# Moving four of sixteen weighted sums per head from TensorE to VectorE in the first token tile of a product-key expert layer

## The reference

```python
def block(xb):                      # 128 tokens at a time
    q = (xb @ w_q).astype(F32).reshape(PEER_BLOCK, PEER_HEADS, 2, half)
    s1 = jnp.einsum("thd,hnd->thn", q[:, :, 0], k1.astype(F32))
    s2 = jnp.einsum("thd,hnd->thn", q[:, :, 1], k2.astype(F32))
...
    idx = jnp.take_along_axis(cand_i, pos, axis=-1)
    g = jax.nn.softmax(top_s, axis=-1)
    u = down[idx]
    act = jax.nn.gelu(jnp.einsum("thkd,td->thk", u, xb).astype(F32), approximate=False)
    return jnp.einsum("thk,thkd->td", (g * act).astype(xb.dtype), up[idx])
```

## Time and profile before

| what | value |
|---|---|
| median of 3 runs | 3074.2 us |
| lowest and highest | 3073.37 and 3075.46 us |
| the profiled execution | 3077.88 us |
| its span (first to last instruction) | 3076.1 us |
| TensorE busy | 2693.7 us, 88% |
| VectorE busy | 1747.6 us, 57% |
| ScalarE busy | 881.3 us, 29% |
| GpSimd busy | 1157.1 us, 38% |
| gathers | 536.90 MB, 41.7% of the span of 16 DMA engines |

### The profile page before, as it was taken

One profiled execution on the slowest core, in us unless ns is written; L12 is line 12 of the kernel. 1 busy time (PEld: TensorE's weight loads), 2 busy tenths in 40 slices (PEclk: granted clock), 3 DMA queues, 4 the chain that ended last, 5 costly groups with the idle time before them and its releaser, 6 DMA issues.

```text
span 3076.1 us, 29817 instructions
## 1 busy us (share of the span) xinstructions
PE 2693.7 (88%) x10970; PEld 1857.5 (60%) x10970; DVE 1747.6 (57%) x3667; ACT 881.3 (29%) x1677; POOL 1157.1 (38%) x763
## 2 busy tenths in 40 slices
PE   6999999989989999899978899988777777777776
PEld 4999899977668888788837755543323233322222
DVE  5666762032747604322175477767777777777665
ACT  3111132134542224222142333333222222222221
POOL 1222233223934444423110355545444444444441
PEclk8999999989999999999988999999999999999999
DMA  6455431212025523212200489999999999999996
GB/s 244 158 182 176 162 127 57 62 62 76 22 69 169 173 96 94 91 62 69 71 0 22 150 339 409 411 427 427 427 427 427 427 427 427 427 427 426 427 427 288
DMA packets 125231, 722.07 MB, mean 235 GB/s; under 512 B 14864, under 2 KB 16144, under 8 KB 58288
## 3 DMA queue, kind: packets, MB, share of 16 engines
q0 software_dynamic: 73728, 536.90, 41.7%
q1 hardware_dynamic: 35920, 127.74, 12.1%
q10 hardware_dynamic: 15456, 55.80, 5.6%
HBM read 718.29 MB, written 2.10 MB: 234 GB/s over the span
## 4 chain that ended last, share of the span: by engine, by line
PE 58%; DMA 27%; DVE 9%; ACT 3%; issue 2%; POOL 1%; SPq 0%; ACTq 0%; DVEq 0%; POOLq 0%
PE acc L619 14%; PE acc L620 14%; PE acc L621 14%; DMA wring<-in_peer_rows,squares 9%; DMA hid<-in_peer_rows,squares 8%; PE sums L1120 5%; DMA arena<-in_peer_rows,squares 4%; DMA resid<-in_peer_rows,squares 3%; PE acc L1120 3%; PE sums L552 1%; DMA modw<-in_peer_rows,squares 1%; DVE hid L2534 1%; DVE squares L1924 1%; ACT hid L1179 1%; PE acc L843 1%
## 5 line engine op out<-in xcount | busy, mean ns | idle before, releaser
L2699 POOL TENSOR_TENSOR wring_parts<-wring,wring_parts 128x1024 fp32r<-128x1024 f32 (+1 forms) x215 | 524.2, 2449 | 1180.8 <-ACT wring_parts L1179 1180.6
L619 PE MATMUL acc<-hid_parts,wring_parts 128*128 128x384 f32 (+1 forms) x2152 | 796.2, 370 | 48.6 <-DVE hid_parts L1871 19.6
L621 PE MATMUL acc<-hid_parts,wring_parts 128*128 128x384 f32 (+1 forms) x2152 | 777.2, 361 | 0.0
L620 PE MATMUL acc<-hid_parts,wring_parts 128*128 128x384 f32 (+1 forms) x1656 | 598.6, 361 | 0.0
L619 PEld LDWEIGHTS acc<-hid_parts,wring_parts 128*128 128x128 f32 x2152 | 407.9, 190 | 116.5 <-issue 50.2
L621 PEld LDWEIGHTS acc<-hid_parts,wring_parts 128*128 128x128 f32 x2152 | 407.5, 189 | 38.5
L1179 ACT ACTIVATE wring_parts<-wring 128x1024 fp32r<-128x1024 f32 (+1 forms) x215 | 223.1, 1040 | 514.0 <-DMA wring<-in_w_ffn_out 196.7
L620 PEld LDWEIGHTS acc<-hid_parts,wring_parts 128*128 128x128 f32 x1656 | 314.9, 190 | 32.9 <-issue 5.5
L2711 POOL DMA_INDIRECT arena<-in_peer_rows,squares x180 | 200.5, 1114 | 244.8 <-PE acc L1120 153.4
L1179 ACT ACTIVATE hid<-hid 128x2 f32<-128x2 f32 (+2 forms) x293 | 67.1, 229 | 764.6 <-DVE arena L2534 237.6
L2711 POOL DMA_INDIRECT wring<-in_peer_rows,squares x158 | 176.7, 1118 | 199.3 <-PE acc L1120 144.2
(11 more groups left out here) (422 smaller groups left out, 4284.1 us busy)
## 6 DMA issues: line engine op xcount, KB each, us to landing
wring<-in_w_ffn_in SPq DMA_DIRECT2D x88, 512.0 KB, 4.7
modw<-in_w_ada ACTq DMA_DIRECT2D x56, 512.0 KB, 3.6
modw<-in_w_mod ACTq DMA_DIRECT2D x48, 512.0 KB, 3.8
wring<-in_w_ffn_out SPq DMA_DIRECT2D x32, 512.0 KB, 3.5
wring<-in_w_in SPq DMA_DIRECT2D x28, 512.0 KB, 3.4
wring<-in_w_mix_in SPq DMA_DIRECT2D x18, 512.0 KB, 3.4
wring<-in_peer_w_q SPq DMA_DIRECT2D x16, 512.0 KB, 5.7
wring<-in_w_ffn_out SPq DMA_DIRECT2D x16, 384.0 KB, 3.1
```

Of the source, the lines that this page charges most:

```text
L619: nc.tensor.matmul(o, wh, high, start=first, stop=False)
L620: nc.tensor.matmul(o, wh, low, start=False, stop=False)
L621: return nc.tensor.matmul(o, wl, high, start=False, stop=last)
L2699: nc.gpsimd.tensor_tensor(Wlor[:, p, 0:blocks, 0:cols], Wlo[:, p, 0:blocks, 0:cols], Whir[:, p, 0:blocks, 0:cols], ALU.subtract).then_inc( ...
```

## The change

Of each head 0 to 6 the picks 1, 5, 9 and 13 (28 picks, the list `BY_VECTOR`) are no longer summed by TensorE. VectorE multiplies the up row by its weight and adds it to a running sum. The first is a `tensor_scalar` that starts the sum, the other 27 are `scalar_tensor_tensor`. The sum of 128x1024 floats lies over constants that this stage no longer reads (from `dup0` on). TensorE and ScalarE skip these 28 picks; the remaining picks are renumbered by `tensor_picks`, for the counts of `diag_ready` and `up_used` and for the choice of the diag buffer. A gather that reuses the pair of such a pick waits for a new semaphore, `vector_used`. After tile 0 `finish` adds VectorE's sum to the PSUM sum in one more instruction.

```diff
+BY_VECTOR = [i * PEER_K + s for i in range(7) for s in (1, 5, 9, 13)]
+def tensor_picks(n):
+    return n - sum(m < n for m in BY_VECTOR)
...
             def weighted(i, first, stop):
...
-                    at = n % SLOTS
-                    pe.wait_ge(diag_ready, n + 1)
+                    if n in BY_VECTOR:
+                        continue
+                    at, d = n % SLOTS, tensor_picks(n)
+                    pe.wait_ge(diag_ready, d + 1)
...
             def expert_weights(i, b):
...
+                    if n in BY_VECTOR:
+                        continue
+                    d = tensor_picks(n)
+                    if d >= N_DIAG:
+                        act.wait_ge(up_used, d - N_DIAG + 1)
...
+            def vector_pick(i, s):
+                n = i * PEER_K + s
+                if n in BY_VECTOR:
+                    k = BY_VECTOR.index(n)
+                    up, weight = pair[PAIR_OF[n]][:, D:2 * D], p_w[:, s:s + 1]
+                    dve.wait_ge(weights_ready, i * (PEER_K // BATCH) + s // BATCH + 1)
+                    if k == 0:
+                        V.tensor_scalar(vector_sum, up, weight, None, ALU.mult).then_inc(vector_used, 1)
+                    else:
+                        dve.wait_ge(vector_used, k)
+                        V.scalar_tensor_tensor(vector_sum, up, weight, vector_sum, ALU.mult, ALU.add).then_inc(vector_used, 1)
...
             def finish(t):
...
+                if t == 0:
+                    dve.wait_ge(vector_used, len(BY_VECTOR))
+                    link(V.tensor_tensor(vector_sum, vector_sum, products, ALU.add))
+                    products = vector_sum
...
                 weights(i, 0)
                 dot(i, 2)
+                vector_pick(i, 1)
...
                 weights(i, 2)
                 dot(i, 6)
+                vector_pick(i, 5)
...
             def gather(n):
...
+                before = PAIR_FREE[n]
+                if before is not None and before in BY_VECTOR:
+                    pool.wait_ge(vector_used, BY_VECTOR.index(before) + 1)
+                elif before is not None:
+                    pool.wait_ge(up_used, tensor_picks(before) + 1)
```

More of the change, by code:

```diff
@@ L124 @@
 MORE_PAIRS = {75: 7, 76: 8, 83: 9, 107: 10, 108: 11, 120: 12}
+BY_VECTOR = [i * PEER_K + s for i in range(7) for s in (1, 5, 9, 13)]
+BY_TENSOR = [_n for _n in range(N_PICKS) if _n not in BY_VECTOR]
+def tensor_picks(n):
+    return n - sum(m < n for m in BY_VECTOR)
 PAIR_OF, PAIR_FREE, PAIR_USE = [], [], []
@@ L130 @@
     PAIR_OF.append(_slot)
-    PAIR_FREE.append(_last.get(_slot, -1) + 1)
+    PAIR_FREE.append(_last.get(_slot))
     PAIR_USE.append(PAIR_OF.count(_slot))
@@ L511, in build @@
         dots_done, gelu_ready, weights_ready = sem("dots_done"), sem("gelu_ready"), sem("weights_ready")
-        diag_ready, up_used = sem("diag_ready"), sem("up_used")
+        diag_ready, up_used, vector_used = sem("diag_ready"), sem("up_used"), sem("vector_used")
+        at = CONST["dup0"][0]
+        vector_sum = cst[:, at:at + D]
         ssq_ready, fstd_ready, fin_ready = sem("ssq_ready"), sem("fstd_ready"), sem("fin_ready")
@@ L1116, in weighted @@
                 for n in range(i * PEER_K + first, i * PEER_K + stop):
-                    at = n % SLOTS
-                    pe.wait_ge(diag_ready, n + 1)
+                    if n in BY_VECTOR:
+                        continue
+                    at, d = n % SLOTS, tensor_picks(n)
+                    pe.wait_ge(diag_ready, d + 1)
                     for hf in range(2):
-                        mm = nc.tensor.matmul(o[:, hf, :], diag[n % N_DIAG], pair[PAIR_OF[n]][:, D + hf * 512:D + (hf + 1) * 512],
+                        mm = nc.tensor.matmul(o[:, hf, :], diag[d % N_DIAG], pair[PAIR_OF[n]][:, D + hf * 512:D + (hf + 1) * 512],
                                               start=(at == 0), stop=(at == SLOTS - 1))
@@ L1734, in expert_weights @@
                 for n in range(first, first + BATCH):
-                    if n >= N_DIAG:
-                        act.wait_ge(up_used, n - N_DIAG + 1)
-                    run(diag[n % N_DIAG], ident, ACT.Copy, scale=p_w[:, n % PEER_K:n % PEER_K + 1]).then_inc(diag_ready, 1)
+                    if n in BY_VECTOR:
[3 more added lines that the diff above has]
+                        act.wait_ge(up_used, d - N_DIAG + 1)
+                    run(diag[d % N_DIAG], ident, ACT.Copy, scale=p_w[:, n % PEER_K:n % PEER_K + 1]).then_inc(diag_ready, 1)
             def final_std(t):
@@ L2550, in finish @@
                     emptied(dve, UNIT["rows"] + w)
-                dve.wait_ge(up_used, (t + 1) * SLOTS)
-                V.tensor_tensor(sum_, total[:, :, :].rearrange("p a n -> p (a n)"), g2row,
-                                ALU.mult).then_inc(tile_read, 1)
+                dve.wait_ge(up_used, tensor_picks((t + 1) * SLOTS))
+                products = total[:, :, :].rearrange("p a n -> p (a n)")
+                if t == 0:
+                    dve.wait_ge(vector_used, len(BY_VECTOR))
+                    link(V.tensor_tensor(vector_sum, vector_sum, products, ALU.add))
+                    products = vector_sum
+                V.tensor_tensor(sum_, products, g2row, ALU.mult).then_inc(tile_read, 1)
                 dve.wait_ge(tile_read, CREDIT + t + 1)
@@ L2600, in head @@
                 dot(i, 10)
+                vector_pick(i, 9)
                 if more:
@@ L2614, in head @@
                 dot(i, 14)
+                vector_pick(i, 13)
                 if more:
@@ L2629, in first_head @@
                 dot(0, 2)
+                vector_pick(0, 1)
                 best_pairs(1)
@@ L2643, in first_head @@
                 dot(0, 6)
+                vector_pick(0, 5)
                 key_numbers(1)
@@ L2656, in first_head @@
                 dot(0, 10)
+                vector_pick(0, 9)
                 best_pairs(2)
@@ L2670, in first_head @@
                 dot(0, 14)
+                vector_pick(0, 13)
                 key_numbers(2)
@@ L2708, in gather @@
                     pool.wait_ge(idx_ready, n // PEER_K + 1)
-                if PAIR_FREE[n]:
-                    pool.wait_ge(up_used, PAIR_FREE[n])
+                before = PAIR_FREE[n]
[3 more added lines that the diff above has]
+                    pool.wait_ge(up_used, tensor_picks(before) + 1)
                 nc.gpsimd.indirect_dma_start(pair[PAIR_OF[n]], None, a["peer_rows"],
```

## The result

The changed kernel is slower: its median is 3090.89 us (3085.75 to 3095.99, 9 runs) against 3074.2 us. The ratio over all runs is 1.0049 with a 95% interval of 1.0033 to 1.0064, so 15 us (the two medians lie 16.7 us apart). The forecast was 3072 us, within 0.2%, range to 3079. It was wrong in sign and in size.

What follows compares the result with a forecast made beforehand. The prediction took DMA to bound the kernel, with only DMA time lost before 2000 us winnable. 3077.9 us (profiled) - 3 + 1 = 3075.9, with profiling 3.7 us above the median, so 3072 us, range 3064 to 3079.

Steps and rivals of the forecast that it cites:

- Only lost DMA time can be won: Before 2000 us: DMA paces everything later, so at most 9.0 us in head 0 and 5.6 us behind it.
- are nearly tied: Heads 1 to 3: per head TensorE needs 41.0 us and DMA 41.8 us.
- the waits of GpSimd for TensorE: 1775 to 2000 us: GpSimd waited 86.9 us for pairs TensorE had not yet freed, so DMA starved.
- TensorE, 3 us won: Behind head 0: 28 picks at 1.72 us taken off TensorE win 3 us, bounds 0 to 5.6.
- Head 0, 1 us lost: Head 0: sums delay dots and diags, 1 us lost; bounds 9.0 us won and 4.9 us lost.
- The query that was to cover sum 9: Head 0: diags delayed by sums 5 and 9 cost nothing while query 6 or 7 covers them for 5.87 us.
- Heads 1 to 3, where the 3 us were to be won: Heads 1 to 3: smaller backlog behind the second query, VectorE's idle time hiding most of its 4.9 us per head.
- Heads 4 to 6 and `finish`, 0: Late heads and the final addition: 12 sums, 15 us, and one 1.22 us addition hidden by VectorE's room, cost 0.
- The price of a sum: VectorE, each sum: 1.22 us, about 4.0 us when meeting a low part of GpSimd, one or two more meetings.
- VectorE takes the place of TensorE: Heads 0 to 3: sums delay dots, gelus, diags and gathers; 3085 us, or 3080 at half; chance 0.12.
- One sign of being wrong: After 2000 us: any stretch with DMA below 427 GB/s would show the forecast wrong.
- The sign of the slow rival: Behind 1850 us: DMA below 411 GB/s with VectorE above 90% busy would show VectorE as the bound.

Runs made afterwards that it cites:

- e2_removed: The 28 picks left out of TensorE and ScalarE with no VectorE sums, against the kernel before: ratio 1.0001 (0.9986 to 1.0016).
- e5_filler: The change plus two unused 128x512 products on TensorE in place of each moved pick, against the kernel before: ratio 1.0006 (0.9987 to 1.0025).
- e8_heads4to6: The change for heads 4 to 6 only (12 picks), against the kernel before: ratio 1.0018 (1.0004 to 1.0033).
- e1_added: VectorE's 28 sums added, results unused, while TensorE and ScalarE keep all picks, against the kernel before: ratio 1.0019 (1.0004 to 1.0034).
- e3_late: The change with each sum moved behind the next odd dot, before the wait for gelu, against the kernel before: ratio 1.0029 (1.0017 to 1.0040).
- e12_before_warm: The kernel before, without sums, plus four 128x512 products on TensorE right before pick 0, against the kernel before: ratio 1.0005 (0.9993 to 1.0017).

## Why the prediction was wrong, point by point

- **The bound.** "Only lost DMA time can be won" held: the time moved as DMA's rates did. That TensorE and DMA "are nearly tied" and that the waits of GpSimd for TensorE are waits for its *work* was wrong. `e2_removed` took away 48 us of that work and won nothing that shows; 36 of the 48 us turned into waits for diags. The 86.9 us of the earlier trace rows name TensorE because it signals last; what it waited for itself was the diag.
- **TensorE, 3 us won.** The step that failed first. 28 x 1.72 us supposed that the other picks keep their 1.72 us; the sum had no term for the clock at all. The granted clock from 1775 to 1850 fell from 0.97 to 0.90, and busy time by 24.7 us only. The gain measured with the sums away is 0 (1.0001). What the relief would win at an unchanged clock no run shows for the whole stage; in the turns of head 6 it was 1.0 us.
- **Head 0, 1 us lost.** It was 5.5 us, in four profiles, just beyond the bound of 4.9 that I gave. The mechanism was named rightly (TensorE waits for diags, so it is not the last to be ready), but a waiting engine was taken for one that costs nothing. The waits of 1.11 and 1.15 us grew to 3.90 and 2.38 us, and the picks behind them ran below full clock. The query that was to cover sum 9 did not: query 7 ended before pick 8, and TensorE then stood 3.90 us in front of pick 10. Of the 4.7 us between the change and `e5_filler`, 3.0 are a later start of pick 14, which goes back to the slow picks 2 and 3 and a piece of the search in head 0 that took 2.60 us instead of 1.61, and 1.7 are the slow pick 14. With the clock restored head 0 loses 0.8 us (`e5_filler`), which is what I had priced.
- **Heads 1 to 3, where the 3 us were to be won.** Gathers 23 to 71 took 131.8 instead of 130.3 us. The scatter between executions is as large as 5 us, so neither a gain nor a loss is shown there.
- **Heads 4 to 6 and `finish`, 0.** This was the second failed step. I read VectorE's busy share (70%) and DMA's 427 GB/s as cover. But in heads 5 and 6 VectorE, ScalarE and TensorE work in turns, and none of VectorE's idle time lies where the sum lies. Each sum is a link of 1.20 us in its turn, and slow picks add to it (1.7 us in one of three turns); in all 0.18% (`e8_heads4to6`). The earlier trace rows averages 2000 to 2500 us and could not show it.
- **The price of a sum**: 1.22 us taken, 1.28 measured; 0.91 to 1.22 for the first, 0.74 measured. One met a low part of GpSimd and took 3.41 us, where the prediction had one or two such meetings at about 4.0. That term was right, and it was not what decided.
- **The rival.** "VectorE takes the place of TensorE", 3080 to 3085 us at 0.12, is nearest to what happened. It too had no clock in its price, and the measured 3090.9 us lie beyond it. Some two fifths of the loss are its mechanism (0.19% in `e1_added`, interval 0.04 to 0.34); the rest needs both.
- **The signs.** One sign of being wrong came in full, a rate below 427 GB/s behind 2000 us (421). The sign of the slow rival came in half: the rate behind 1850 us fell below 411 (405), but VectorE was 82% busy there (122.87 of 150 us) and not above 90%. A loss through VectorE did not need a full VectorE.

Two things stay open. In head 6 the chain shows the clock as the whole difference that the filler makes. For the rest of the stage, heads 1 to 5 above all, that the clock is the only way in which a standing TensorE acts is not shown. And when a wait costs the pick behind it its speed is not settled: 2.83 us did not in `e2_removed` and in `e3_late` (1.99 us at pick 10), nor 2.85 us in the change, while 2.38 us did in the change.

## What to carry to other kernels

An engine that others wait for is not the bound if it waits itself: take its work away in one run, before moving it anywhere. Work taken off TensorE can come back as a lower clock for what is left, and that costs most where another engine has just lost the idle time in which it would have caught up. And before an instruction is called hidden by idle time, find in the chain of waits where that idle time lies; engines that work in turns have it only where the new instruction is not.

## What the runs showed of the hardware

- TensorE ran the picks behind waits of about 1.1 us in 1.98 us or less. Behind waits of 2.4 to 4.8 us some took 2.7 to 3.8 us, at a granted clock of 0.53 over pick 14, and others 1.98 us: behind 2.82 and 2.85 us in the change, behind 2.83 and 2.86 us in `e2_removed`. Pick 0 took 3.75 us behind a wait of 3.74, and 1.98 us with four useless products right before it (`e12_before_warm`).
- 56 useless products of 128x512 on TensorE (54 us busy in the trace of `e5_filler`), in a kernel of 3.1 ms, made the changed kernel 0.43% faster.
- One `tensor_scalar` of 128x1024 floats between SBUF addresses took 0.74 us on VectorE where the form with two tensors took 1.28 us.
